# Turning the hidden blocks of five feed-forward layers on TensorE instead of VectorE and ScalarE

## The chip, the cores and the metric

The kernel runs on one core of one Trainium2 chip. The metric is the device time of one execution in microseconds (us): the median over the runs of a kernel. One further execution is recorded by the hardware profiler; its span is what the rows below count in.

## The reference, cut to what matters

Two transformer blocks of two layers each run one after the other on a sequence of 256 tokens with a width of 1024. Five times on the way stands the same gated feed-forward with a hidden width of 2816, all in float32:

```python
def swiglu_ffn(x, g, w_gate, w_up, w_down):
    h = rmsnorm(x, g)
    return (jax.nn.silu(h @ w_gate) * (h @ w_up)) @ w_down
```

The first block adds half of it to `x`, four times (two layers, ahead of and behind each mixer); the second block has it once, in its first layer. The second layer of the second block has a mixture of experts in its place. Between them stand mixers (attention and recurrences), which this change does not touch.

## The kernel before, in words

The whole network is one program. Each stage is a phase with a program written out by hand for every engine; semaphores order the engines, and a barrier of all engines ends a phase. `feed_forward` is called five times. It cuts the hidden width into 11 groups of 256 (`total = FF_PAIRS = 11`), and does two things.

**Gate and up.** For a group `c` both projections together are one block product of a 2 by 2 split: token halves (rows 0 to 127 and 128 to 255) by halves of the 1024 inputs, times input halves by (gate, up). It is done with seven products in place of eight (`P1` to `P7`), for which VectorE makes sums of weight blocks (`sum_up`, L990: four of 128x1024 for each group) and later adds the results up. Each product is four matmuls of 128 by 128 on 256 columns; each such float32 matmul is two instructions in the trace (so 8 to a product and 56 to a group, all at L878). For c > 0 the order is `P1 P6 P5 P7 P2 P4 P3`.

What the engines hand each other in a group: ScalarE copies P1 to `p1` (L941); VectorE forms `u2 = p1 + P6` (`sum_u2`, L1044), which TensorE waits for ahead of P2; `v = P7 + u2` and `up1 = P5 + v` (`sum_up1`, L1049 and L1051), which TensorE waits for ahead of P3; then in `finish` gate1 (L1055), hidden1 (L1057), up0 (L1059) and hidden0 (L1061). Hidden1 and hidden0 are silu(gate) * up, 128 tokens by 256 hidden units each, in the two halves of the tile `up`.

**The turn.** The down projection needs the hidden blocks with the hidden units on the partitions: four blocks of 128 by 128 to a group. VectorE turns the tile `up` in blocks of 32 by 32 (L1065, one instruction of 128x512), which leaves each small block turned but in its old place; ScalarE puts them into `hT` with 16 copies of a strip of 32 partitions (`place_blocks`, L931), behind its copy of P1 of the next group. Then VectorE makes four sums of turned blocks (`mix_hidden`, L1016).

**Down.** A second block product of seven products: for each of 11 groups seven matmuls on 512 columns, two instructions each (L898), summed over the groups in seven PSUM banks. Bank 7 (`TURN_BANK`) is used in the fifth feed-forward alone, by a small side product (`half_on_tensor`) at groups 1 to 4.

Weights come by DMA from the queue of SyncE, 2 MB to a group for gate and up; a slot is refilled once TensorE has finished the group that used it. TensorE transposes of 128 by 128 float32 stand elsewhere in the kernel already: at the end of a feed-forward and at the start of the next phase (`turn_block`, L658, four to a block), and in the mixers (L1576, L2261, L3150); each is one instruction in the trace.

The order of VectorE's work in a group c > 0, in which the sums are those for the next group:

```python
                sums_behind(c, 0)
                sums_behind(c, 1)
                sum_u2(c)
                sums_behind(c, 2)
                sums_behind(c, 3)
                dve.wait_ge(turned, c)
                sum_up1(c)
                mix_hidden(c - 1)
                finish(c)
```

Of the kernel before, what the change touches and what calls it, by code (L numbers as in the profile page):

```python
# [24 lines left out]
ACT = mybir.ActivationFunctionType  # L25
AX = mybir.AxisListType.X

P = 128
# [6 lines left out]
GROUP = 256  # L35
# [723 lines left out]
def feed_forward(prog, weights, gain, factor=1.0, after=(), side=None, loads=None, meanwhile=None, fresh=False, exit_gain=None, then="rows", last_norm=None):  # L759
# [11 lines left out]
    u2, v, first_gate, gate1, p1 = (mem.take(GROUP) for _ in range(5))  # L771
    up, silu, up_blocks = (mem.take(2, GROUP) for _ in range(3))
    p1_wide, u2_wide, v_wide = (Arena(prog, temps_at + i * BANK).take(BANK) for i in range(3))
# [14 lines left out]

    strip = lambda n: slice(32 * n, 32 * (n + 1))
    first_half, last_half = slice(0, KT // 2), slice(KT // 2, KT)  # L790
# [4 lines left out]
    def hidden_of(g):  # L795
        blocks = {"11": hT[:, g, 0, :], "12": hT[:, g, 1, :], "21": hT[:, g, 2, :], "22": hT[:, g, 3, :]}
        blocks.update({f"S{i + 1}": hT[:, g, 4 + i, :] for i in range(4)})
        return blocks
# [7 lines left out]
    with prog.phase() as ph:  # L806
        made, turned, acc_made, pair_used = (ph.semaphore(n) for n in ("made", "blocks_turned", "acc_made", "pair_used"))
        x_mixed_done, summed, posted, first_posted = (
# [37 lines left out]
        def _(pe):  # L846
            def gate_up(c, name):
# [32 lines left out]
                last.then_inc(made, 1)  # L880

            def down(g, name):
                left, right = factors[name]
                if g == 0:
                    if name == "P1":
                        pe.wait_ge(silu_ready, 2 * total - 1)
                    elif name == "P4":
                        pe.wait_ge(posted, posted_at(total - 1, "gate1"))
                    elif name == "P3":
                        pe.wait_ge(posted, posted_at(total - 1, "up0"))  # L890
                if name == "P1":
                    weights.wait(pe, weights.down + g)
                    pe.wait_ge(copied, g + 1)
                if name in SUM_OF:
                    pe.wait_ge(down_summed, 4 * g + SUM_OF[name])
                if name in MIX_OF:
                    pe.wait_ge(mixed, 4 * g + MIX_OF[name])
                return pe.matmul(psum[:, DOWN_BANK[name], :], hidden_of(g)[left], down_weights(g)[right],  # L898
                                 start=(g == 0), stop=(g == total - 1), skip_group_check=True)
# [5 lines left out]
            for c in range(total):  # L905
                for name in order_of(c):
                    gate_up(c, name)
            for g in range(total - 2):
                for name in PRODUCTS:
                    last = down(g, name)  # L910
                last.then_inc(pair_used, 1)
                if side and 1 <= g <= 4:
                    side.half_on_tensor(pe, g - 1, TURN_BANK)
# [11 lines left out]
        def _(act):  # L925
            def place_blocks(c):
                act.wait_ge(turned, c + 1)
                of = up_blocks.rearrange("p i (f n) -> p (i f) n", f=2)
                for m in range(4):
                    for j in range(4):  # L930
                        last = act.activation(hT[strip(m), c, 0:4, strip(j)], of[strip(j), :, strip(m)], ACT.Copy)  # L931
                last.then_inc(copied, 1)

# [5 lines left out]
            for c in range(total):  # L939
                act.wait_ge(made, made_at(c, "P1"))  # L940
                act.activation(p1, psum[:, UP_BANK["P1"], 0:GROUP], ACT.Copy).then_inc(p1_copied, 1)  # L941
                if c:
                    place_blocks(c - 1)
                    act.wait_ge(made, made_at(c, "P2"))
                    act.activation(silu[:, 0, :], psum[:, UP_BANK["P2"], 0:GROUP], ACT.Silu, scale=prog.rstd[:, 0:1]).then_inc(silu_ready, 1)
                else:
                    act.wait_ge(first_posted, 1)
                    act.wait_ge(entry.ready, 1)
                    act.activation(silu[:, 0, :], first_gate, ACT.Silu, scale=prog.rstd[:, 0:1]).then_inc(silu_ready, 1)
                act.wait_ge(posted, posted_at(c, "gate1"))  # L950
                act.activation(silu[:, 1, :], gate1, ACT.Silu, scale=prog.rstd[:, 1:2]).then_inc(silu_ready, 1)
            place_blocks(total - 1)
            if meanwhile:
# [15 lines left out]
        def _(dve):  # L969
# [83 lines left out]
            def finish(c):  # L1053
# [7 lines left out]
                dve.scalar_tensor_tensor(up[:, 0, :], up[:, 0, :], prog.rstd[:, 0:1], silu[:, 0, :], ALU.mult, ALU.mult).then_inc(posted, 1)  # L1061
                dve.wait_ge(posted, posted_at(c, "hidden0"))
                if c:
                    dve.wait_ge(copied, c)
                dve.transpose(up_blocks.rearrange("p i n -> p (i n)"), up.rearrange("p i n -> p (i n)")).then_inc(turned, 1)  # L1065

# [8 lines left out]
            for c in range(1, total):  # L1075
                sums_behind(c, 0)
                sums_behind(c, 1)
                sum_u2(c)
                sums_behind(c, 2)
                sums_behind(c, 3)  # L1080
                dve.wait_ge(turned, c)
                sum_up1(c)
                mix_hidden(c - 1)
                finish(c)
# [3487 lines left out]
```

## Time and profile before

| | |
|---|---|
| median of 3 runs | 3235.86 us (3235.29 to 3240.46) |
| time of the profiled execution | 3235.86 us |
| its span in the trace | 3234.0 us |
| mean granted TensorE clock | 0.993 of full speed |
| busy share of the span: TensorE, VectorE, ScalarE | 98%, 43%, 25% |
| gate and up, five stretches | from 11.2, 397.0, about 600, 939.8 and 1566.8 us, some 134 to 138 us each |
| down, five stretches | from 147.7, 531.4, 735.0, 1074.2 and 1705.2 us, some 66 to 75 us each |

The time of the profiled execution lies 1.9 us above its span and equals the median. In rows of the timeline the first number is the start, the second the length, both in us; instructions that follow each other are merged with their count. The length runs to the end of the last one; since matmuls overlap, what a row costs TensorE is the start of the next row less its own start. A bracket gives idle time ahead of the row and what ended it. In rows of groups, the number behind the bar is the busy time and the mean ns of one; behind the second bar stands the idle time of the engine just ahead of them.

### The profile page before, as it was taken

The numbers are of one execution on the slowest core, as the hardware profiler recorded it, in microseconds if no ns is written. First come the engines' busy times: TensorE is split into PE (matmuls) and PEld (weight loads), VectorE is DVE, ScalarE is ACT, GpSimd is POOL, SyncE is SP. The second block draws the span as 40 slices with busy tenths as digits, with TensorE's granted clock in tenths as the row PEclk, the third lists the DMA queues.
The fourth block names the chain that finished last, engine by engine and source line by source line (L and its number), as shares of the span: only waits on it lengthen the run. The fifth ranks groups of instructions, "written<-read, shape, count | busy, mean of one in ns | idle before, by whom it ended". The sixth has DMA issues, their size and how long they took to land. (4 is left out here: it accounts for less than half of the span.)

```text
span 3234.0 us, 46425 instructions
## 1 busy us (share of the span) xinstructions
PE 3157.3 (98%) x18957; PEld 1845.5 (57%) x18957; DVE 1392.8 (43%) x2513; ACT 807.6 (25%) x2139; POOL 169.0 (5%) x157
## 2 busy tenths in 40 slices
PE   8999999999999999999999999999999999999999
PEld 7845686685568567785684586864333333333333
DVE  7743386775447545633575336432112111212122
ACT  4413343351234243221352233232100000000000
POOL 0001000000000002300001104010100000000000
PEclk9999999999999999999999999999999999999999
DMA  7542045344424440134344511142899999899993
GB/s 292 195 157 105 27 160 218 131 172 161 163 75 166 182 177 27 66 115 153 153 172 153 188 56 65 54 179 87 347 382 401 393 399 399 342 393 400 392 401 134
DMA packets 81042, 665.51 MB, mean 206 GB/s; under 512 B 10528, under 2 KB 11168, under 8 KB 14016
## 3 DMA queue, kind: packets, MB, share of 16 engines
q1 hardware_dynamic: 80400, 661.31, 52.5%
q8 instruction: 152, 2.49, 0.3%
q10 hardware_dynamic: 432, 1.24, 0.1%
q14 instruction: 58, 0.48, 0.0%
HBM read 661.46 MB, written 1.05 MB: 205 GB/s over the span
## 5 line engine op out<-in xcount | busy, mean ns | idle before, releaser
L4078 PE MATMUL psum<-ring,arena 128*32 128x512 f32 x5376 | 587.8, 593 | 0.0
L878 PE MATMUL psum<-ring,arena 128*128 128x256 f32 x1760 | 398.4, 379 | 2.0 <-DVE arena L977 1.1
L4078 PEld LDWEIGHTS psum<-ring,arena 128*32 128x32 f32 x5376 | 172.3, 110 | 389.6 <-issue 388.7
L878 PEld LDWEIGHTS psum<-ring,arena 128*128 128x128 f32 x1760 | 333.8, 190 | 48.9 <-DVE ring L990 3.1
L878 PE MATMUL psum<-ring,xT_norm 128*128 128x256 f32 x1320 | 305.0, 381 | 8.9 <-DVE arena L1044 7.3
L4110 PE MATMUL psum<-ring,arena 128*32 128x512 f32 x2688 | 293.6, 592 | 0.7 <-DVE arena L4246 0.7
L878 PEld LDWEIGHTS psum<-ring,xT_norm 128*128 128x128 f32 x1320 | 251.1, 191 | 45.2 <-issue 9.2
L931 ACT ACTIVATE arena<-arena 32x128 f32<-32x128 f32 x880 | 269.5, 306 | 27.3 <-DVE arena L1065 17.7
L990 DVE TENSOR_TENSOR ring<-ring 128x1024 f32<-128x1024 f32 x220 | 266.8, 1215 | 13.2 <-DMA ring<-in_ffn_w 6.8
L4242 DVE TENSOR_TENSOR arena<-arena,psum 128x256 f32<-128x256 f32 x84 | 35.5, 423 | 411.0 <-ACT arena L4216 411.0
L898 PE MATMUL psum<-ring,arena 128*128 128x512 f32 x440 | 205.8, 592 | 0.0
L4110 PEld LDWEIGHTS psum<-ring,arena 128*32 128x32 f32 x2688 | 88.2, 110 | 200.5 <-issue 191.2
L2972 PE MATMUL psum<-xT_norm,ring 128*128 128x256 f32 x832 | 184.4, 380 | 0.0
L4254 DVE TENSOR_TENSOR arena<-arena,psum 128x512 f32<-128x512 f32 x156 | 107.7, 690 | 157.4 <-PE psum L4110 157.4
L2972 PEld LDWEIGHTS psum<-xT_norm,ring 128*128 128x128 f32 x832 | 157.1, 190 | 25.3 <-issue 4.9
L898 PE MATMUL psum<-arena 128*128 128x512 f32 x330 | 157.9, 592 | 0.0
L898 PEld LDWEIGHTS psum<-ring,arena 128*128 128x128 f32 x440 | 83.3, 190 | 101.2 <-issue 100.9
L4216 ACT ACTIVATE arena<-psum 128x256 f32<-128x256 f32 x84 | 32.5, 386 | 420.7 <-PE psum L4078 420.7
L4188 ACT ACTIVATE arena<-psum 128x384 f32<-128x384 f32 x28 | 13.8, 493 | 419.7 <-PE psum L4091 419.7
L898 PEld LDWEIGHTS psum<-arena 128*128 128x128 f32 x330 | 62.4, 190 | 77.0 <-issue 76.3
L1001 DVE TENSOR_TENSOR arena<-ring 128x512 f32<-128x512 f32 x55 | 40.0, 728 | 122.0 <-PE psum L898 122.0
L3666 PE MATMUL psum<-ring,xT_norm 128*128 128x256 f32 (+1 forms) x256 | 84.6, 486 | 0.0
(594 smaller groups left out, 3504.0 us busy)
## 6 DMA issues: line engine op xcount, KB each, us to landing
ring<-in_moe_w SPq DMA_DIRECT2D x340, 1024.0 KB, 7.2
ring<-in_ffn_w SPq DMA_DIRECT2D x50, 2048.0 KB, 7.6
ring<-in_ffn_w SPq DMA_DIRECT2D x65, 1024.0 KB, 4.9
ring<-in_merge_w SPq DMA_DIRECT2D x16, 2048.0 KB, 8.3
ring<-in_feat_w SPq DMA_DIRECT2D x12, 2048.0 KB, 8.7
ring<-in_ev_in_w SPq DMA_DIRECT2D x4, 2048.0 KB, 9.0
ring<-in_od_in_w SPq DMA_DIRECT2D x4, 2048.0 KB, 9.4
ring<-in_merge_w SPq DMA_DIRECT2D x8, 1024.0 KB, 11.6
```

The costliest lines, as they stand in the source:

```text
L878: last = pe.matmul(psum[:, bank, 0:GROUP], a[:, k, :], w[:, k, :], start=(fresh and k == 0), stop=(k == KT // 2 - 1), skip_group_check=True)
L898: return pe.matmul(psum[:, DOWN_BANK[name], :], hidden_of(g)[left], down_weights(g)[right], start=(g == 0), stop=(g == total - 1), skip_gr ...
L931: last = act.activation(hT[strip(m), c, 0:4, strip(j)], of[strip(j), :, strip(m)], ACT.Copy)
L990: dve.tensor_tensor(w[out], w[a], w[b], ALU.subtract).then_inc(summed, 1)
L1001: dve.tensor_tensor(w[out], w[a], w[b], ALU.subtract).then_inc(down_summed, 1)
L2972: last = pe.matmul(psum[:, s % 4, x * S:(x + 1) * S], weights[:, i, (f + x) * P:(f + x + 1) * P], prog.xT[:, i, :], start=(i == 0), stop=( ...
L3666: last = pe.matmul(gate_bank(m)[:, at:at + w.shape[2]], prog.xT[:, k, b * P:(b + 1) * P], w[:, k, :], start=(k == 0), stop=(k == KT - 1))
L4078: last = pe.matmul(psum[part(j), r, :], xg[:, u.i, u.group // GROUPS, r * P + BLOCK * j:r * P + BLOCK * (j + 1)], m[:, j, :], start=(u.i = ...
L4110: last = pe.matmul(psum[part(j), down_bank(n, r), :], hT[:, c, r * P + BLOCK * j:r * P + BLOCK * (j + 1)], m[:, j, :], start=(c == 0), sto ...
L4216: act.activation(silu[:, r, :], psum[:, r, 0:S], ACT.Silu).then_inc(silu_ready, 1)
L4242: dve.tensor_tensor(hidden[:, r, :], silu[:, r, :], psum[:, r, S:2 * S], ALU.mult).then_inc(hidden_ready, 1)
L4254: last = dve.tensor_tensor(at, at, psum[:, down_bank(n, r), :], ALU.add)
```

## The change

The turn moves to TensorE. For each group `turn(c)` transposes the four blocks of `up` into bank 7 with four TensorE transposes, and one ScalarE copy of 128x512 (`copy_turned`) takes them to `hT`. The turn of group c - 1 stands behind P6 of group c; that of the last group stands behind the fourth product (P7) of the first down group. VectorE's block transpose, the 16 strip copies of ScalarE and the tile `up_blocks` go. The wait on `copied`, which guarded `up_blocks`, now guards bank 7. In VectorE's order `mix_hidden(c - 1)` moves ahead of the fourth sum and of `sum_up1`. The blocks "12" and "21" of `hT` change places, since the copy keeps the order of the transposes. In the fifth feed-forward TensorE also waits for the last copy out of bank 7 before the side product uses it.

```diff
-    up, silu, up_blocks = (mem.take(2, GROUP) for _ in range(3))
+    up, silu = mem.take(2, GROUP), mem.take(2, GROUP)
...
-        blocks = {"11": hT[:, g, 0, :], "12": hT[:, g, 1, :], "21": hT[:, g, 2, :], "22": hT[:, g, 3, :]}
+        blocks = {"11": hT[:, g, 0, :], "21": hT[:, g, 1, :], "12": hT[:, g, 2, :], "22": hT[:, g, 3, :]}
...
+            def turn(c):
+                pe.wait_ge(posted, posted_at(c, "hidden0"))
+                if c:
+                    pe.wait_ge(copied, c)
+                for t in range(2):
+                    for i in range(2):
+                        last = pe.transpose(psum[:, TURN_BANK, (2 * t + i) * P:(2 * t + i + 1) * P], up[:, i, t * P:(t + 1) * P],
+                                            prog.ident)
+                last.then_inc(turned, 1)
...
                 for name in order_of(c):
                     gate_up(c, name)
+                    if c and name == "P6":
+                        turn(c - 1)
             for g in range(total - 2):
-                for name in PRODUCTS:
+                for n, name in enumerate(PRODUCTS):
                     last = down(g, name)
+                    if g == 0 and n == 3:
+                        turn(total - 1)
                 last.then_inc(pair_used, 1)
+                if side and g == 1:
+                    pe.wait_ge(copied, total)
...
-            def place_blocks(c):
+            def copy_turned(c):
                 act.wait_ge(turned, c + 1)
-                of = up_blocks.rearrange("p i (f n) -> p (i f) n", f=2)
-                for m in range(4):
-                    for j in range(4):
-                        last = act.activation(hT[strip(m), c, 0:4, strip(j)], of[strip(j), :, strip(m)], ACT.Copy)
-                last.then_inc(copied, 1)
+                act.activation(hT[:, c, 0:4, :].rearrange("p j t -> p (j t)"), psum[:, TURN_BANK, :], ACT.Copy).then_inc(copied, 1)
...
                 if c:
-                    place_blocks(c - 1)
+                    copy_turned(c - 1)
...
-                dve.wait_ge(posted, posted_at(c, "hidden0"))
-                if c:
-                    dve.wait_ge(copied, c)
-                dve.transpose(up_blocks.rearrange("p i n -> p (i n)"), up.rearrange("p i n -> p (i n)")).then_inc(turned, 1)
...
                 sum_u2(c)
                 sums_behind(c, 2)
+                mix_hidden(c - 1)
                 sums_behind(c, 3)
-                dve.wait_ge(turned, c)
                 sum_up1(c)
-                mix_hidden(c - 1)
                 finish(c)
```

## Rows read from the trace of the kernel before

**Rows 1.** The page, granted TensorE clock in 40 slices of the span, tenths.

```profile
PEclk9999999999999999999999999999999999999999
```

**Rows 2.** Costliest groups by line, whole span: gate and up, strip copies, block transpose.

```profile
L878 PE MATMUL psum<-ring,arena 128*128 128x256 f32 x1760 | 398.4, 379 | 2.0 <-DVE arena L977 1.1 <-DVE ring L990 0.9
...
L878 PE MATMUL psum<-ring,xT_norm 128*128 128x256 f32 x1320 | 305.0, 381 | 8.9 <-DVE arena L1044 7.3 <-DMA ring<-in_ffn_w 1.6
...
L931 ACT ACTIVATE arena<-arena 32x128 f32<-32x128 f32 x880 | 269.5, 306 | 27.3 <-DVE arena L1065 17.7
...
L1065 DVE STREAM_TRANSPOSE arena<-arena 128x512 f32<-128x512 f32 x55 | 39.1, 711 | 1.9
```

**Rows 3.** Timeline, second feed-forward, group 2 to the start of group 3.

```profile
422.65 1.89 PE L878 MATMUL psum<-ring,xT_norm 128*128 128x256 f32 x8
...
423.31 0.49 DVE L1061 SCALAR_TENSOR_TENSOR arena<-arena,norm_stats 128x256 f32<-128x256 f32 x1
...
424.37 5.34 PE L878 MATMUL psum<-ring,arena 128*128 128x256 f32 x24
...
429.55 3.62 PE L878 MATMUL psum<-ring,xT_norm 128*128 128x256 f32 x16
...
434.73 1.46 PE L878 MATMUL psum<-ring,xT_norm 128*128 128x256 f32 x6
```

**Rows 4.** Timeline, TensorE around the four transposes in the first feed-forward's end.

```profile
208.60 0.60 PE L658 MATMUL psum<-constants,x_resid 128*128 128x128 f32 x4
209.04 3.60 PE L898 MATMUL psum<-ring,arena 128*128 128x512 f32 x8
```

**Rows 5.** Timeline, TensorE around 32 transposes in a mixer, and what follows.

```profile
1295.89 3.66 PE L3150 MATMUL psum<-constants,ring 128*96 128x128 f32 x32
1300.66 1.13 PE L2187 MATMUL psum<-arena 64*128 64x256 f32 x8 [1.11 <-PEq L377]
```

**Rows 6.** Windows: length, TensorE busy and instructions, granted clock, DMA share, GB/s.

```profile
1300.00:1305.00 5.00, 4.34 (x33) 1.00 0.69 244
...
1590.00:1592.00 2.00, 2.00 (x6) 0.50 0.00 0
```

**Rows 7.** Timeline, four transposes between short products in a mixer.

```profile
1349.34 0.66 PE L2261 MATMUL psum<-constants,ring 128*128 128x128 f32 x4
1350.11 0.59 PE L2221 MATMUL psum<-arena 128*128 128x192 f32 x2
```

**Rows 8.** Timeline, second feed-forward, group 1.

```profile
410.86 5.34 PE L878 MATMUL psum<-ring,arena 128*128 128x256 f32 x24
410.92 0.49 DVE L1061 SCALAR_TENSOR_TENSOR arena<-arena,norm_stats 128x256 f32<-128x256 f32 x1
...
412.07 4.84 DVE L990 TENSOR_TENSOR ring<-ring 128x1024 f32<-128x1024 f32 x4
...
416.83 0.41 DVE L1044 TENSOR_TENSOR arena<-arena,psum 128x256 f32<-128x256 f32 x1
...
417.39 3.69 PE L878 MATMUL psum<-ring,xT_norm 128*128 128x256 f32 x16 [1.19 <-DVE arena L1044]
...
420.01 0.42 DVE L1051 TENSOR_TENSOR arena<-psum,arena 128x256 f32<-128x256 f32 x1
420.35 1.14 DVE L1016 TENSOR_TENSOR arena<-arena 128x128 f32<-128x128 f32 x4
420.92 1.89 PE L878 MATMUL psum<-ring,arena 128*128 128x256 f32 x8
```

**Rows 9.** Timeline, fifth feed-forward, group 1.

```profile
1582.97 0.49 DVE L1061 SCALAR_TENSOR_TENSOR arena<-arena,norm_stats 128x256 f32<-128x256 f32 x1
...
1588.88 0.42 DVE L1044 TENSOR_TENSOR arena<-arena,psum 128x256 f32<-128x256 f32 x1
...
1589.44 5.38 PE L878 MATMUL psum<-ring,xT_norm 128*128 128x256 f32 x16 [2.08 <-DVE arena L1044]
1594.66 1.67 PE L878 MATMUL psum<-ring,arena 128*128 128x256 f32 x7
```

**Rows 10.** Timeline, fifth feed-forward's side product: ScalarE copy of a PSUM bank.

```profile
1719.10 0.60 ACT L4399 ACTIVATE arena<-psum 128x512 f32<-128x512 f32 x1 [6.92 <-PE psum L4392]
```

More of the change, by code:

```diff
@@ L787, in down_weights @@
         return {"11": w[:, 0, 0], "12": w[:, 0, 1], "21": w[:, 1, 0], "22": w[:, 1, 1], "T1": s1, "T2": s2, "T3": w[:, 0, 1], "T4": s4}
-    strip = lambda n: slice(32 * n, 32 * (n + 1))
     first_half, last_half = slice(0, KT // 2), slice(KT // 2, KT)
@@ L806, in feed_forward @@
     with prog.phase() as ph:
-        made, turned, acc_made, pair_used = (ph.semaphore(n) for n in ("made", "blocks_turned", "acc_made", "pair_used"))
+        made, turned, acc_made, pair_used = (ph.semaphore(n) for n in ("made", "hidden_turned", "acc_made", "pair_used"))
         x_mixed_done, summed, posted, first_posted = (
@@ L951, in _ @@
                 act.activation(silu[:, 1, :], gate1, ACT.Silu, scale=prog.rstd[:, 1:2]).then_inc(silu_ready, 1)
-            place_blocks(total - 1)
+            copy_turned(total - 1)
             if meanwhile:
```

## The prediction, made before the changed kernel ran

> **What bounds the kernel now.** I read the page first, for the shares and the clock; then the groups by line, for what ended TensorE's idle time in the feed-forwards; then the timeline of one feed-forward, for the order inside a group; then rows of transposes elsewhere, for the price of a turn. The granted clock is at nine tenths or more of full speed in every slice [rows 1]. In gate and up, TensorE issued 3080 instructions (1760 and 1320) and sat idle for only 2.0 + 8.9 = 10.9 us ahead of them, over all five feed-forwards; 7.3 us of this were ended by VectorE's u2 at L1044 [rows 2]. The reader should see how little there is to win there. A settled group shows it from inside: P1 of group 2 starts at 422.65 and P1 of group 3 at 434.73, so a group takes 12.08 us; the first product takes 424.37 - 422.65 = 1.72 us, and seven of these are 12.06 us [rows 3]. TensorE does not stop within a group, and this holds for the groups behind it too, since the 7.3 us are five waits, one in each feed-forward, all in group 1 (1.65, 1.19, 1.19, 1.18 and 2.08 us; two of the five stand in [rows 8, 9]). The down products follow the same way without a stop.
>
> So VectorE's block transpose (55 of 0.711 us) and the 880 strip copies of ScalarE (269.5 us in all) [rows 2] lie beside TensorE's work, except where they push u2 of group 1 back. What is put on TensorE, on the other hand, lies on the path.
>
> **What is added to TensorE.** Eleven turns in each of five feed-forwards, 55 in all, of four transposes: 220 instructions. The kernel has the same four transposes between two runs of matmuls: they start at 208.60, the next matmul at 209.04 [rows 4]. A turn therefore takes 0.44 us of TensorE, or 0.11 us for a transpose. The length of one in that row (0.60 us for four) contains a tail that overlaps with the next matmul and is not paid. Thirty-two in a row took 3.66 us with the tail [rows 5], 0.11 each again. For a lower bound I take 0.43 (a quarter of the product's 1.72 us, since a turn streams 512 columns once where a product streams 1024 twice); for an upper one the widest that four transposes have between short products in a mixer, 1350.11 - 1349.34 = 0.77 us [rows 7], where some of it may be a wait. I take 0.44, since those neighbours are long matmul runs as here. 55 x 0.44 = 24.2 us.
>
> The Trainium skill ("TensorE: Matmul & The Clock Gate", Part 4: PE-mode transpose) gives about 275 ns for a 128x128 transpose inside a kernel. By that the 220 would be an estimated 60 us. The spacing in the rows above speaks for the smaller number: the page's figure is near the length of a single one here, not near the distance to the next.
>
> **Does the turn wait?** It needs hidden0 of the group before, posted at 423.31 + 0.49 = 423.80; P6 ends at 424.37 + 1.72 = 426.09 [rows 3]. It has 2.3 us to spare, and the wait costs nothing. If it were late, P5 and all behind it would be. The copy out of bank 7 is long done by the next turn.
>
> **ScalarE.** Sixteen strips of 0.306 us, 4.9 us a group, become one copy from PSUM of 0.60 us [rows 10]. Nothing on TensorE waited for the strips, so this is worth nothing but free time.
>
> **VectorE.** The transpose goes; this frees 412.07 - 411.41 = 0.66 us ahead of the sums, of which 0.03 stay as the usual gap: 0.63. In a settled group it buys nothing. `mix_hidden` now stands ahead of the fourth sum. It waits for the copied blocks: turn until 426.53, about 0.2 for the signal, 0.60 for the copy, 427.3. VectorE gets there after u2 (from about 426.3, for 0.41) and a sum of 1.21 (a quarter of 4.84 [rows 8]), at 427.9. Behind it stand the fourth sum and v and up1, for which P3 waits: 427.9 + 1.05 + 1.21 + 0.45 + 0.42 = 431.1, but v needs P7 (out at 426.53 + 3.44 + 0.2 = 430.2), so about 431.1 either way; P3 is due at 426.53 + 4 x 1.72 = 433.4. It is 2.3 us early. The move is free there.
>
> **Group 1, where VectorE is late.** In the second feed-forward P7 of group 1 ends at 410.86 + 3 x 1.72 = 416.0, and P2 starts at 417.39, behind u2 (posted 417.24) [rows 8]. After the change: P6 ends at 412.58, hidden0 was posted at 411.41, the turn runs to 413.02, P7 ends at 416.46. VectorE's four sums start at 411.44; u2 starts 0.63 earlier, at 416.20, is posted at 416.61, and P2 starts at 416.76. The turn is hidden in the old wait, and 0.63 us more is gained. But next comes P3, which waits for up1. VectorE: sum until 417.75, mix_hidden occupying 421.40 - 420.35 = 1.05 until 418.8, sum until 420.0, v and up1 until 420.87, so P3 starts at 421.02 instead of 420.92 [rows 8]; TensorE would be ready at 416.76 + 3.53 = 420.29. The moved mix_hidden gives the gain back as a new wait of 0.7 us. Net for group 1: +0.10 us instead of +0.44. From group 2 on VectorE has caught up. A feed-forward costs 10 x 0.44 + 0.10 = 4.5 us; four cost 18.0.
>
> **The fifth.** There the first weights came late, and TensorE idled enough for its granted clock to fall to 0.50, that is 1.2 GHz, just behind the wait of 2.08 us [rows 6, 9]: the 16 instructions of P2 and P4 took 1594.66 - 1589.44 = 5.22 us where they take 3.53 in [rows 8]. With the turn, TensorE works until about 1587.5 (turn behind hidden0, 1583.46 + 0.15 + 0.44, then P5 and P7), and P2 starts 0.64 earlier, at 1588.8: an idle of 1.3 us, about that of the feed-forwards in which the clock held. I take it that it holds. Then P3 waits for up1, 4.26 us behind u2 as in group 1 above: 1588.66 + 4.26 + 0.15 = 1593.1, which is 1.6 earlier. If the clock falls all the same, 0.6 earlier. So 4.4 - 1.6 = 2.8 us.
>
> **Sum.** 18.0 + 2.8 = +20.8 us on the profiled execution of 3235.86, which is also the median: 3256.7 us. Queues are not passed: no DMA is added or moved, SyncE starts each weight load behind the same products, and loads start later with TensorE itself. The last turn stands in the first down group, behind the fourth product. A down product streams half the columns of one of gate and up, so four are 4 x 0.86 = 3.4 us behind the last P3, while hidden0 comes 1.15 us behind it (423.80 less 422.65 [rows 3]); the turn does not wait. The added wait of the side product is for a copy many us old.
>
> **The rivals.**
>
> A. A turn costs more than 0.44 (switching from matmuls to transposes and back, loading `up` as weights between short matmuls of 256 columns). For: in a mixer four took 0.77 [rows 7]. Against: [rows 4]. At 0.77: (50 x 0.77) + 0.5 - 1.6 = 37 us, 3273 us. Halfway, 0.60: 28.5 us, 3264.
>
> B. The clock suffers. If transposes did not keep the clock up, the turn and the wait of group 1 would together let it fall in the other four feed-forwards as in the fifth, at 5.22 - 3.53 = 1.7 us each, and in the fifth as well, where 1.0 us of the gain is lost: +7.8, 3264.5 us. Against: 32 transposes alone, from 1295.89, with 1.11 us of idle behind them, left the clock at 1.00 in the next 5 us [rows 5, 6]. The Trainium skill ("TensorE: Matmul & The Clock Gate", Part 4) says that the full clock does not engage for transposes, which do not count as busy in the same way; by that rule this rival would hold, and the trace does not agree with it.
>
> C. The other side: not slower. TensorE's time is regained from somewhere. The waits of group 1 are worth 7.3 us, all counted; even with all 10.9 us of idle gone, 24.2 - 10.9 = +13.3. Only the clock is large enough: a mean of 0.993 over 3234 us is 22.6 us that could at most be missing. If the shifted phases met no low clock anywhere, the time would be 24.2 - 22.6, about 3237.5 us; it decides from 14.4 regained beyond my sum. Against: the low stretches lie nearly all in mixers, which the change only moves.
>
> D. Milder: `mix_hidden` early does not delay up1 in group 1, so that P3 follows at once: -0.7 in each, 3253.2 us.
>
> **How the numbers follow.** My forecast 0.70; A 0.10; B 0.04; C 0.05; D 0.11. 0.2% of the median is 6.5 us, about what a measurement of this kernel can tell from no change. The forecast, A, B and D are slower: 0.95. C lies within 0.2% at its own price, but reaches to both sides of it. I give 0.93 to slower, 0.05 to the same and 0.02 to faster, which leaves 0.02 for the low end of the others, should a turn and the clock both come out cheap. The range: down to D and a further 3 us for clock phases, 3250; up to the half-way case of A and B, 3265.
>
> **What the profile after would show.** 220 TensorE instructions at the new transpose line, started about 0.11 us apart, and the product behind each turn 0.44 us after it began; groups of 12.5 us in place of 12.08; no row of the block transpose, 55 ScalarE copies of some 0.6 us; the idle ended by L1044 down from 7.3 us to about 2 us, and a new one of about 0.7 us in each group 1 ended by the up1 line; in the fifth feed-forward no stretch at 0.50. The prediction is wrong if the gap of a turn is clearly above or below 0.44, if P5 or P3 waits in settled groups, or if stretches outside the feed-forwards change their length by several us.

## The result, and the profile after

| | before | after |
|---|---|---|
| median, runs side by side | 3239.0 us (5 runs, 3235.29 to 3241.51) | 3267.56 us (5 runs, 3257.35 to 3277.86) |
| profiled execution, its span | 3235.86, 3234.0 us | 3268.03, 3266.2 us |
| mean granted clock of that execution | 0.993 | 0.990 |
| busy TensorE, VectorE, ScalarE (page) | 3157.3, 1392.8, 807.6 us | 3192.1, 1358.0, 575.7 us |

The ratio is 1.0088, with a 95% interval of 1.0058 to 1.0116. The change makes the kernel slower, as forecast, but by more than the range allowed: 3267.56 lies above 3265. With these five runs the record holds thirteen more executions of the kernel after; all eighteen have a median of 3267.4 us.

The groups by line of the kernel after answer to [rows 2]. The new instructions are the transposes (L887) and the 55 copies of a bank (L943); the gate and up product stands at L877 now.

```profile
L877 PE MATMUL psum<-ring,arena 128*128 128x256 f32 x1760 | 406.7, 379 | 2.2 <-DVE arena L1062 1.7 <-DVE ring L1001 0.5
L877 PE MATMUL psum<-ring,xT_norm 128*128 128x256 f32 x1320 | 304.9, 381 | 3.0 <-DMA ring<-in_ffn_w 1.7 <-DVE arena L1055 1.3
...
L887 PE MATMUL psum<-constants,arena 128*128 128x128 f32 x220 | 33.1, 273 | 0.3 <-DVE arena L1072 0.3
...
L943 ACT ACTIVATE arena<-psum 128x512 f32<-128x512 f32 x55 | 32.9, 597 | 112.2 <-PE psum L887 112.2
```

The wait for u2 (now L1055) fell from 7.3 to 1.3 us; the one for up1 (L1062), 1.7 us, is new. The timeline of the second feed-forward, from P6 of group 1 to P6 of group 3, answers to [rows 3, 8]:

```profile
416.34 1.89 PE L877 MATMUL psum<-ring,arena 128*128 128x256 f32 x8
...
418.06 0.60 PE L887 MATMUL psum<-constants,arena 128*128 128x128 f32 x4
418.50 3.62 PE L877 MATMUL psum<-ring,arena 128*128 128x256 f32 x16
...
421.58 0.41 DVE L1055 TENSOR_TENSOR arena<-arena,psum 128x256 f32<-128x256 f32 x1
...
422.14 3.69 PE L877 MATMUL psum<-ring,xT_norm 128*128 128x256 f32 x16
423.05 1.14 DVE L1027 TENSOR_TENSOR arena<-arena 128x128 f32<-128x128 f32 x4
...
425.69 0.42 DVE L1062 TENSOR_TENSOR arena<-psum,arena 128x256 f32<-128x256 f32 x1
...
426.17 1.99 PE L877 MATMUL psum<-ring,arena 128*128 128x256 f32 x8 [0.34 <-DVE arena L1062]
...
428.00 1.89 PE L877 MATMUL psum<-ring,xT_norm 128*128 128x256 f32 x8
...
429.73 1.89 PE L877 MATMUL psum<-ring,arena 128*128 128x256 f32 x8
...
431.45 0.60 PE L887 MATMUL psum<-constants,arena 128*128 128x128 f32 x4
431.89 3.62 PE L877 MATMUL psum<-ring,arena 128*128 128x256 f32 x16
...
442.25 1.89 PE L877 MATMUL psum<-ring,arena 128*128 128x256 f32 x8
```

The turn takes 431.89 - 431.45 = 0.44 us, and a group 442.25 - 429.73 = 12.52 us in place of 12.08. Group 1 hides its turn: from P6 (416.34) to the next P1 (428.00) it is 11.66 us, where it was 422.65 - 410.86 = 11.79.

Stage by stage, from the first and the last TensorE row of each stage in the two traces:

| us | before | after | difference |
|---|---|---|---|
| gate and up, five feed-forwards | 136.42, 134.38, 134.38, 134.37, 138.39 | 139.94, 138.21, 138.22, 138.22, 141.15 | +17.8 |
| down, five | 67.13, 67.13, 67.13, 66.26, 74.00 | 67.57, 67.57, 67.57, 66.69, 74.44 | +2.2 |
| first and second mixer | 182.26, 137.70 | 183.57, 142.73 | +6.3 |
| between fourth and fifth feed-forward | 426.35 | 429.36 | +3.0 |
| start; behind the fifth | 11.24; 1449.94 | 11.44; 1452.56 | +2.8 |

The lengths are from this one trace of each kernel. The feed-forwards, where all of the change is, account for 20.0 us of the 32.2. The other 12.2 us came in stages whose code did not change. The windows show what part of that is (length, busy time and instructions of TensorE, weight loads, VectorE, ScalarE, GpSimd, granted clock, DMA share, GB/s). The kernel after, in its second mixer:

```profile
916.00:918.00 2.00, 2.00 (x11) 2.00 (x11) 0.00 (x0) 1.19 (x2) 0.00 (x0) 0.50 0.04 8
918.00:920.00 2.00, 2.00 (x12) 2.00 (x11) 0.00 (x0) 0.00 (x0) 0.00 (x0) 0.50 0.00 0
```

The kernel before, at the same work:

```profile
902.00:904.00 2.00, 2.00 (x21) 2.00 (x20) 0.00 (x0) 0.94 (x2) 0.00 (x0) 1.00 0.04 8
```

The two timelines show that the work and the idle time ahead of it are alike. Before, then after:

```profile
901.19 1.07 PE L1269 MATMUL psum<-constants,arena 128*128 128x128 f32 x8 [1.14 <-ACT arena L1358]
902.10 3.68 PE L1282 MATMUL psum<-arena 128*128 128x64 f32 x32
```

```profile
915.32 1.75 PE L1275 MATMUL psum<-constants,arena 128*128 128x128 f32 x8 [1.14 <-ACT arena L1364]
916.85 6.93 PE L1288 MATMUL psum<-arena 128*128 128x64 f32 x32
```

The same 1.14 us of idle, the same 40 instructions: once at full clock, once at half. I summed (1 - granted clock) over windows of 2 us through both traces: 23.6 us lost before, 31.8 after. The losses come in pieces of 1.7 us or multiples. The second mixer has one piece before (1.7 us) and 6.8 us after. So 8.2 us of the growth between these two traces is low clock, net of 1.7 us that the fifth feed-forward gained.

### The profile page after: what moved, and what is told of

Its sections match the earlier page's. It is cut to its first block and busy times, and to the rows that moved or that the text cites. A ratio compares the mean times of both kernels' runs of the same rounds, so it can differ in the third digit from the quotient of the medians.

```text
span 3266.2 us, 45985 instructions
## 1 busy us (share of the span) xinstructions
PE 3192.1 (98%) x19177; PEld 1873.0 (57%) x19177; DVE 1358.0 (42%) x2458; ACT 575.7 (18%) x1314; POOL 169.1 (5%) x157
## 3 DMA queue, kind: packets, MB, share of 16 engines
HBM read 661.46 MB, written 1.05 MB: 203 GB/s over the span
## 5 line engine op out<-in xcount | busy, mean ns | idle before, releaser
L877 PE MATMUL psum<-ring,arena 128*128 128x256 f32 x1760 | 406.7, 379 | 2.2 <-DVE arena L1062 1.7
L877 PEld LDWEIGHTS psum<-ring,arena 128*128 128x128 f32 x1760 | 330.0, 190 | 47.2 <-DVE arena L1062 3.7
L877 PE MATMUL psum<-ring,xT_norm 128*128 128x256 f32 x1320 | 304.9, 381 | 3.0 <-DMA ring<-in_ffn_w 1.7
L877 PEld LDWEIGHTS psum<-ring,xT_norm 128*128 128x128 f32 x1320 | 251.0, 191 | 39.6 <-issue 3.2
L907 PE MATMUL psum<-ring,arena 128*128 128x512 f32 x440 | 206.6, 592 | 0.0
L2978 PEld LDWEIGHTS psum<-xT_norm,ring 128*128 128x128 f32 x832 | 156.7, 190 | 25.2 <-issue 4.6
L4222 ACT ACTIVATE arena<-psum 128x256 f32<-128x256 f32 x84 | 32.4, 386 | 420.7 <-PE psum L4084 420.7
L3711 PE MATMUL psum<-ring,arena 128*128 128x512 f32 x192 | 83.2, 593 | 0.0
```

What stands on the lines that cost most here:

```text
L877: last = pe.matmul(psum[:, bank, 0:GROUP], a[:, k, :], w[:, k, :], start=(fresh and k == 0), stop=(k == KT // 2 - 1), skip_group_check=True)
L2978: last = pe.matmul(psum[:, s % 4, x * S:(x + 1) * S], weights[:, i, (f + x) * P:(f + x + 1) * P], prog.xT[:, i, :], start=(i == 0), stop=( ...
L3711: last = pe.matmul(branch_bank(n), oT[:, turned_order.index(x), k, b * P:(b + 1) * P], w[:, j, k, :], start=(k == 0), stop=(k == 3))
```

## The experiments

The questions: is the price inside the feed-forwards the turn's; is the rest tied to the turn, to any delay, or to chance; and was there a time to be had from the wait for u2. In the table the third column is the ratio to the kernel before on the same chip with its 95% interval.

| kernel | median us (runs) | ratio | before beside it |
|---|---|---|---|
| before again | 3243.02 (12) | 1.0018 [0.9996, 1.0041] | 3238.91 (20) |
| after again, 1st | 3269.17 (6) | 1.0105 [1.007, 1.0139] | 3238.91 |
| after again, 2nd | 3268.33 (6) | 1.0078 [1.0063, 1.0094] | 3241.0 (17) |
| after again, 3rd | 3270.46 (6) | 1.0105 [1.0069, 1.0142] | 3238.13 (23) |
| turns alone | 3263.99 (9) | 1.0069 [1.0042, 1.0095] | 3238.91 |
| mix_hidden put back | 3269.53 (6) | 1.009 [1.0061, 1.0118] | 3238.91 |
| one transpose for four | 3248.47 (12) | 1.0022 [1.0007, 1.0037] | 3241.0 |
| delay of 1.7 us in one place | 3245.12 (12) | 1.0012 [0.9993, 1.003] | 3239.34 (24) |
| delay of 3.5 us in one place | 3244.96 (11) | 1.002 [1.001, 1.0029] | 3239.34 |
| delay of 20 us in one place | 3259.67 (5) | 1.0072 [1.0058, 1.0086] | 3239.34 |
| the same again | 3260.74 (10) | 1.0062 [1.0042, 1.0081] | 3238.13 |
| delay of 4.1 us in each feed-forward | 3266.64 (6) | 1.0081 [1.0059, 1.0103] | 3241.0 |
| the same again | 3262.13 (8) | 1.0071 [1.0038, 1.0104] | 3238.13 |
| u2 early in group 1 | 3227.01 (6) | 0.9966 [0.9955, 0.9978] | 3239.34 |
| the same again | 3231.24 (12) | 0.997 [0.9952, 0.9989] | 3238.13 |
| GpSimd later by one memset | 3269.16 (8) | 1.0104 [1.006, 1.0148] | 3240.9 (9) |
| GpSimd later by six memsets | 3266.92 (6) | 1.0091 [1.006, 1.0121] | 3241.47 (11) |

### The two kernels again

> The kernel before, unchanged, for the spread of its time. Theory P (the feed-forwards cost what the turns cost, some 20 us, and the rest of the 28 us comes from where the granted clock falls to one half in stages that the change does not touch): the runs of this kernel scatter as well, by several pieces of 1.7 us, and time less the time lost to the half clock is constant within 1 us. Theory S (something in the change makes the untouched stages slower): all runs stay within 3235 to 3242 us.

> The changed kernel, unchanged, for its spread and a second trace. Theory P: the stretches of gate and up and of down have the same lengths as in the first trace (138.2 and 67.6 us, within 0.2), and the untouched stages have other lengths than in it, by pieces of 1.7 us. Theory S: the untouched stages are again about 12 us longer than in the kernel before, in the same places.

> The changed kernel once more, for the spread, beside the pure delay on the same chip. Median 3265 to 3269 if what was seen holds; 3260 to 3263 if the earlier medians were high by luck.

> The changed kernel once more beside both delays: mean of the kernel before plus 26 to 28.

Both medians came back. The stretches of gate and up and of down repeated within 0.02 us in the second to fourth feed-forward and within 0.4 us in the first; the first mixer took 182.26 and 185.04 us in two executions of the kernel before, and 183.57, 189.09, 179.03 and 188.98 in four of the kernel after. The scatter of a run is thus outside the feed-forwards, in the mixers for the most part; once, in the second repeat, the stretch behind the fifth feed-forward took 17 us more. All 121 runs of the kernel before together have a median of 3240.9 us and reach from 3231.2 to 3266.3, and the three runs shown ahead of the prediction were 5 us below that median. The 36 executions of the kernel after (the eighteen of the result and three repeats of six) have 3268.9. The third repeat was expected 26 to 28 us above the kernel before; by its mean it was 32.9 us above it on the same chip.

### The turns alone

This is the kernel before, with its block transpose and strip copies; the transposes go to bank 7, where nobody reads them.

```diff
+            def turn(c):
+                pe.wait_ge(posted, posted_at(c, "hidden0"))
+                for t in range(2):
+                    for i in range(2):
+                        pe.transpose(psum[:, TURN_BANK, (2 * t + i) * P:(2 * t + i + 1) * P], up[:, i, t * P:(t + 1) * P],
+                                     prog.ident)
...
+                    if c and name == "P6":
+                        turn(c - 1)
```

> The kernel before with the 55 turns added on TensorE at the same places, their result unused; VectorE's block transpose and ScalarE's strips stay. Theory P: 54 or so settled turns of 0.44 us; in group 1 the turn hides in the wait for u2. Each feed-forward grows by 10 x 0.44 = 4.4 us, 22 in all, 3258 us give or take the clock; no group shorter. Rival (the changed time is made by the moved VectorE and ScalarE work): under 10 us.

The down group got the same turn behind its fourth product. The timeline of this kernel, around the turn of group 1 in the second feed-forward:

```profile
424.22 0.60 PE L886 MATMUL psum<-constants,arena 128*128 128x128 f32 x4
424.65 3.62 PE L878 MATMUL psum<-ring,arena 128*128 128x256 f32 x16
...
429.01 3.69 PE L878 MATMUL psum<-ring,xT_norm 128*128 128x256 f32 x16 [0.74 <-DVE arena L1055]
```

The turn is 0.43 us again, and the old wait for u2 shrinks from 1.19 to 0.74 us by the length of the turn. A feed-forward (second to fourth) became 3.95 + 0.44 = 4.4 us longer; the change's own are 3.84 + 0.44 = 4.3. So the turns on TensorE make the price inside the feed-forwards. The rest of the change has two parts there that nearly cancel, as the next kernel shows.

### mix_hidden put back behind sum_up1

An edit of the kernel after:

```diff
-                mix_hidden(c - 1)
                 sums_behind(c, 3)
                 sum_up1(c)
+                mix_hidden(c - 1)
```

> The changed kernel with mix_hidden back behind sum_up1. The wait of P3 in group 1 goes (0.34 us and 0.1 at the restart), since up1 no longer stands behind mix_hidden: each feed-forward 0.4 us shorter, 2 us in all, hidden in the scatter of the total but to be seen in the stretches: gate and up 137.8 us instead of 138.2. If mix_hidden's move were what makes the change dear, 5 us or more would go.

The timeline of this kernel, group 1 of the second feed-forward from the turn on:

```profile
413.69 0.60 PE L887 MATMUL psum<-constants,arena 128*128 128x128 f32 x4
414.13 3.62 PE L877 MATMUL psum<-ring,arena 128*128 128x256 f32 x16
...
417.77 3.69 PE L877 MATMUL psum<-ring,xT_norm 128*128 128x256 f32 x16
...
421.30 1.89 PE L877 MATMUL psum<-ring,arena 128*128 128x256 f32 x8
```

P3 follows P4 at once; the wait of 0.34 us is gone, and gate and up takes 137.61 us in place of 138.21. The moved `mix_hidden` costs 0.6 us in each of these feed-forwards, where 0.4 was expected: P3 starts 3.53 us behind P2 in place of 4.03, and the next P1 1.73 us behind P3 in place of 1.83. Without the move a feed-forward would be (137.61 - 134.38) + 0.44 = 3.7 us dearer than before, against 4.4 with the turns alone. So taking the transpose off VectorE gave 0.7 us back in group 1, and the move of `mix_hidden` spent 0.6 of it. The median did not fall with it: its 3 us drown in the mixers' scatter at six runs.

### One transpose in place of four

For every group but the first of a feed-forward the turn holds one transpose. This kernel leaves out the other three, so three of the four hidden blocks of such a group are not turned; the waits are unchanged. An edit of the kernel after:

```diff
-                for t in range(2):
-                    for i in range(2):
+                for t in range(1 if c else 2):
+                    for i in range(1 if c else 2):
```

> The changed kernel with one transpose in place of four in every turn but the first of a feed-forward; the other three blocks of each are left as they were, so this part of the hidden values is not computed. ScalarE's copy, VectorE's order and all waits stay. If the transposes are the cost, 50 x 3 x 0.11 = 16 us go: a settled group of 12.19 us instead of 12.52, 3252 us against 3268. If the switch between matmuls and transposes, or the wait, is the cost, little goes, and a turn still takes 0.3 us or more.

The timeline of this kernel, the turn in a settled group:

```profile
433.93 0.27 PE L887 MATMUL psum<-constants,arena 128*128 128x128 f32 x1
434.04 3.62 PE L877 MATMUL psum<-ring,arena 128*128 128x256 f32 x16
```

A lone transpose between long products takes 434.04 - 433.93 = 0.11 us, a quarter of 0.44: the rows show no cost of switching. The five feed-forwards are 16.1 us shorter in this trace than with four transposes, where 50 x 3 x 0.11 = 16.5 were expected; the median fell by 20.4 us from the 3268.9 of the kernel after, and the rest of that is within the scatter. The length of the lone transpose in its row is 0.27 us.

The Trainium skill ("TensorE: Matmul & The Clock Gate", Part 4: PE-mode transpose) gives about 275 ns, measured with bf16; in these float32 rows this is near the length, while the distance to the next instruction, 0.11 us, is what TensorE pays.

### Delays without the change

Filler matmuls on zeros into the free bank 7, by the kernel's own function `stay_busy`, are put into the kernel before behind P7 of the first down group: 8, 16 and 93 of them in the second feed-forward alone, then 19 in each of the five (without the last condition of the edit shown, and in the first behind a wait for the constants' load). Their result is not used.

```diff
-                for name in PRODUCTS:
+                for n, name in enumerate(PRODUCTS):
                     last = down(g, name)
+                    if g == 0 and n == 3 and weights is prog.shifted:
+                        stay_busy(prog, pe, TURN_BANK, 8)
```

> The kernel before with 8 small matmuls (128x512, bf16, of zeros) put in once, behind the fourth product of the first down group of the second feed-forward, before all the mixers but the first: a pure delay of 8 x 0.216 = 1.7 us, no other work changed. Theory P (where the granted clock falls depends on when a stage comes, and on luck from run to run): the later stages keep their work and idle, but pieces of 1.7 us come and go in them; time less 1.7 lies between 3232 and 3264 with a median that may be some us off 3241. Theory S (the later stages are slower in the changed kernel because of its turns): median 3242.5, the later stages as in the kernel before.

> The same with 16 matmuls, a delay of 3.5 us. Theory P as for 1.7 us. Theory S: median 3244.5.

> The same with 93 matmuls, a delay of 20.1 us, the size of what the turns cost in the feed-forwards. If the 7 to 10 us above the turns' price come with any delay of this size, the median is 3266 to 3270 as in the changed kernel; if they hang on the turns or the freed engines, it is 3259 to 3262; if luck alone made them, either.

> The delay of 20.1 us in one place once more. Mean of the kernel before plus 20 to 22 if the first five runs hold; plus 24 or more if they were low by luck and any late mixer pays.

> The kernel before with a pure delay of 19 x 0.216 = 4.1 us in each of the five feed-forwards, 20.5 in all, behind the fourth product of the first down group, so that every later stage comes about as late as in the changed kernel. If the 6 to 7 us that the changed kernel has above its feed-forwards' 20 come from when the mixers come (where the clock falls), the median is 3266 to 3270; if they hang on the transposes or on the freed engines, or are luck of the runs, it is 3260 to 3263.

> The pure delay of 4.1 us in each feed-forward once more, for a mean over twice as many runs. If the time above the delay comes with the delay itself, the mean stays 4 to 8 us above that of the kernel before plus 20.5; if the first six runs were high by luck, it falls to within 2 us of it.

The traces show the delays at their size: the down stretches grew by 1.73, 3.46, 20.07 and five times 4.10 us. The medians alone leave the matter open: against the kernel before on the same chip they grew by 20.3 and 22.6 us for the 20.1 us in one place, and by 25.6 and 24.0 for the 20.5 in five. Each run also comes with its mean granted clock, and time times clock is the time that it would have taken had no clock been lost. (Low clock behind the last matmul counts here too, though TensorE does nothing there; in the first two traces this is 1.3 and 1.1 us.) The clock is rounded to a thousandth (3.2 us), so only means over many runs count. Means with their standard errors:

| us | runs | mean time | time x clock | lost to low clock |
|---|---|---|---|---|
| before | 116 | 3241.6 | 3211.8 ± 0.1 | 29.8 ± 0.7 |
| after (all on record) | 36 | 3269.5 | 3237.1 ± 0.2 | 32.4 ± 1.5 |
| of these, the three repeats | 18 | 3272.1 | 3237.2 ± 0.3 | 34.9 ± 2.1 |
| turns alone | 9 | 3266.6 | 3236.5 ± 0.4 | 30.2 ± 3.6 |
| 1.7 us in one place | 12 | 3243.9 | 3215.0 ± 0.2 | 28.9 ± 1.2 |
| 3.5 us in one place | 11 | 3245.0 | 3217.5 ± 0.4 | 27.4 ± 1.1 |
| 4.1 us in each feed-forward | 14 | 3265.9 | 3236.0 ± 0.4 | 29.9 ± 2.5 |
| 20.1 us in one place | 15 | 3260.7 | 3235.5 ± 0.4 | 25.2 ± 1.0 |
| u2 early | 18 | 3230.7 | 3205.4 ± 0.3 | 25.3 ± 1.3 |

The change adds 25.3 ± 0.2 us of work and waits at full clock. The feed-forwards account for 20.0 of it and for 1.7 more that the fifth paid before as low clock; 3.6 us lie outside. Pure delays show the same kind of surcharge: 1.7 us put in become 3.2, 3.5 become 5.7, 20.1 become 23.7, and 20.5 become 24.2. So a surcharge of 1.5 to 3.7 us comes with a delay, without any transpose. With the turns alone 2.0 us lie outside. The traces show one place of it: with the low clock taken off, the stretch between the fourth and the fifth feed-forward took 424.6 and 423.3 us in two executions of the kernel before, 425.8 to 426.2 in four of the kernel after, and 425.5 to 427.0 in four with the large delays.

The low clock decides less than the repeats alone suggest. They lost 5.1 ± 2.2 us more than the kernel before; all 36 executions lost 2.6 ± 1.7 us more, which is not clear of zero. The five delays show no difference to the kernel before, the single one of 20.1 us lost 4.6 ± 1.2 less. What makes the clock fall in one execution and not in another is not shown.

### VectorE and GpSimd in the last mixer

One part outside the feed-forwards was the same in all six traces in which VectorE's and ScalarE's part of the turn had been changed and nothing was put ahead of GpSimd's product, and in none of the eleven traces of the kernel before, of the turns alone, of the delays and of the early u2. In the last mixer VectorE and GpSimd each multiply a tile of 128x1536 at the same time. The timeline of the kernel before:

```profile
1947.25 1.76 DVE L3485 TENSOR_TENSOR ring<-ring,arena 128x1536 f32<-128x1536 f32 x1
1947.38 4.24 POOL L3353 TENSOR_TENSOR ring<-ring,arena 128x1536 f32<-128x1536 f32 x1 [37.08 <-DVE arena L3482]
```

The kernel after, with the product of TensorE that waits for VectorE's next step:

```profile
1976.75 2.76 POOL L3359 TENSOR_TENSOR ring<-ring,arena 128x1536 f32<-128x1536 f32 x1 [37.08 <-DVE arena L3488]
1976.96 4.15 DVE L3491 TENSOR_TENSOR ring<-ring,arena 128x1536 f32<-128x1536 f32 x1 [0.46 <-DVE arena L3488]
...
1989.47 3.85 PE L3018 MATMUL psum<-arena,constants 8*128 8x256 f32 x11 [1.32 <-DVE arena L3497]
```

GpSimd is first by 0.21 us here; its product takes 2.76 us instead of 4.24 and VectorE's 4.15 instead of 1.76. TensorE then waits 1.32 us where it waited 0.26. Two kernels put memsets of an unused column ahead of GpSimd's product, to turn the order round, the first with the one line shown, the second with six of it:

```diff
             pool.wait_ge(squared, SQUARES["k"])
+            do(pool.memset(prog.spare, 0.0))
             do(tt(k_mla, k_mla, spread(kept.qk_stat[:, 1].unsqueeze(3), TB, NH8, QK), ALU.mult))
```

> The changed kernel with one tiny GpSimd memset (one column of a spare tile) ahead of GpSimd's product of 128x1536 in the last mixer, so that GpSimd starts it a few tenths of a us later and VectorE's product of the same shape starts first, as in the kernel before. If who starts first decides, VectorE's takes 1.76 us again instead of 4.15, GpSimd's about 4.2 instead of 2.8, TensorE's wait behind it 0.26 instead of 1.32, and the stretch behind the last feed-forward is 1.1 us shorter, 2.8 where a half-clock piece goes with it. If the length comes from something else (where the tiles lie), it stays 4.15.

> The kernel after, with six tiny GpSimd memsets of one unused column ahead of GpSimd's first product in the last mixer (one cost 0.18 us, so GpSimd starts some 0.9 us later than with one). Theory of the start order (whichever of the two starts its product first runs undisturbed, the other is drawn out): VectorE's product takes 1.76 us again in place of 4.15 to 4.31, GpSimd's first product is drawn out from 2.76 to about 4.2 us, TensorE's wait behind the next VectorE step falls from 1.32 to about 0.3 us, and the median falls by 1 us, or by up to 2.8 us if a half-clock piece goes with it (some 3266 to 3268). Rival (VectorE is slow there for another reason, such as what it did before): VectorE's product stays above 4 us although it starts first, TensorE's wait stays 1.3 us, and the median stays at about 3269.

One memset did not do it: GpSimd started at 1973.41, VectorE at 1973.47 and took 4.31 us, so that run said nothing. Six did. The timeline of that kernel:

```profile
1978.02 1.76 DVE L3498 TENSOR_TENSOR ring<-ring,arena 128x1536 f32<-128x1536 f32 x1 [0.46 <-DVE arena L3495]
...
1978.73 3.65 POOL L3366 TENSOR_TENSOR ring<-ring,arena 128x1536 f32<-128x1536 f32 x1
...
1989.46 4.61 PE L3019 MATMUL psum<-arena,constants 8*128 8x256 f32 x16 [0.26 <-DVE arena L3504]
```

VectorE's product is back at 1.76 us, TensorE's wait at 0.26, the low clock behind it at 3.4 us in place of the 5.1 of the kernel after, and everything behind the fifth feed-forward took 1450.56 us against 1452.56. The start order is shown to be the cause of 1.1 us. The 1.7 us of clock went in this one execution, so that part is likely, not shown: of the seven traces with the slow product five lost 5.1 and two 3.4, of the twelve with the quick one none lost more than 3.4. Of the 2.8 us in all, 0.8 came back in small steps elsewhere in the stretch. The median of 3266.92 us is too scattered (3260.45 to 3287.8) to show 2 us. The numbers fit a wait of the second until the first is done: 0.71 us after VectorE's start GpSimd would wait out 1.05 and then need 2.76, 3.81 in all, measured 3.65. In the kernel before the same sum gives 4.39 for GpSimd (measured 4.24), in the kernel after 4.31 for VectorE (4.15), with one memset 4.46 (4.31).

The Trainium skill ("SBUF — State Buffer", section "SBUF: two separate sides") says that a VectorE instruction with two SBUF inputs and a GpSimd one that reads SBUF exclude each other for the whole instruction, and that whichever starts first gets the shared ports; the rows agree to 0.15 or 0.16 us in all four cases.

Why VectorE started 0.46 us behind its reciprocal in the kernels with the changed work of VectorE and ScalarE, and 0.11 in the others, stays open. It is neither the delay nor the transposes, since with either of them alone it was 0.11.

### u2 early in group 1

The prediction had found 7.3 us of waits for u2 in the kernel before. This kernel takes them without moving the turn: in group 1 VectorE makes u2 ahead of the weight sums, and up1 ahead of the last two.

```diff
             for c in range(1, total):
+                if c == 1:
+                    sum_u2(c)
                 sums_behind(c, 0)
                 sums_behind(c, 1)
-                sum_u2(c)
+                if c == 1:
+                    dve.wait_ge(turned, c)
+                    sum_up1(c)
+                else:
+                    sum_u2(c)
                 sums_behind(c, 2)
                 sums_behind(c, 3)
-                dve.wait_ge(turned, c)
-                sum_up1(c)
+                if c > 1:
+                    dve.wait_ge(turned, c)
+                    sum_up1(c)
```

> The kernel before (VectorE's turn) with another order in group 1 alone: u2 ahead of the sums for the next group, v and up1 behind two of them. TensorE's wait for u2 (7.3 us in five places) goes: P2 follows P7 at once, 1.4 us earlier in each of the second to fourth feed-forwards, 1.9 in the first, 2.3 plus 1.7 of clock in the fifth; 9 to 10 us in all, if up1 is in time for P3: 3231 us against 3241, give or take the clock. If VectorE is only late elsewhere instead, under 3 us.

> The kernel before with u2 early in group 1, once more: mean 9 to 12 us below the kernel before.

The timeline of this kernel, group 1 of the second feed-forward, answers to [rows 8]:

```profile
405.82 5.34 PE L878 MATMUL psum<-ring,arena 128*128 128x256 f32 x24
...
409.39 0.41 DVE L1044 TENSOR_TENSOR arena<-arena,psum 128x256 f32<-128x256 f32 x1
...
411.00 3.62 PE L878 MATMUL psum<-ring,xT_norm 128*128 128x256 f32 x16
```

P2 follows P7 without a wait. Gate and up became 132.96 us from 134.38 in three feed-forwards, 134.94 from 136.42 in the first, and 134.21 from 138.39 in the fifth, where the half-clock stretch of [rows 6] went too: 9.9 us, and the mean over 18 runs fell by 10.9: 6.4 us at full clock and 4.5 as low clock. It beats both kernels.

## Why the prediction was right and where it failed

**The turn's price** was right: 0.44 us, 220 transposes 0.11 apart, groups of 12.52 us, the last turn in the down group 0.43 or 0.44. Rival A (0.77, or 0.60) is refuted by the timeline and by the kernel with one transpose.

**Group 1** was right in kind. The turn is hidden, u2's wait nearly went, and a wait for up1 came, of 0.34 us where 0.7 was worked out; VectorE's path from P6 to the end of up1 took 9.77 us in place of 10.01, and P3 followed up1 by 0.06 us in place of 0.15. P3 starts 9.83 us behind P6 (426.17 - 416.34), not 10.16. The group gained 0.13 where it was to lose 0.10. So the group came out 0.23 us better than forecast, a third of the 0.7 of rival D. Putting `mix_hidden` back shows that its move costs 0.6 us in a feed-forward; in settled groups it is free, as said.

**The fifth feed-forward**: +2.76 and +0.44 = 3.2, where 2.8 was forecast. Its clock held behind P2's wait of 1.10 us, as this row and these windows of the kernel after show:

```profile
1615.68 3.69 PE L877 MATMUL psum<-ring,xT_norm 128*128 128x256 f32 x16 [1.10 <-DVE arena L1055]
```

```profile
1614.00:1616.00 2.00, 0.90 (x5) 0.50 (x4) 2.00 (x3) 0.00 (x0) 0.00 (x0) 1.00 0.02 8
1616.00:1618.00 2.00, 2.00 (x11) 1.77 (x10) 1.93 (x6) 0.32 (x1) 0.00 (x0) 1.00 0.00 0
```

A turn waited there once, for 0.25 us (the 0.3 at L887). Rival B is refuted: no window of a feed-forward of the kernel after is below full clock.

**The sum over the feed-forwards**, +20.8, measured +20.0. This part of the sum held to 0.8 us.

**What failed first is the base.** The sum was added to 3235.86, "the profiled execution ... which is also the median". Three runs close together looked like a sharp base; 121 runs have a median of 3240.9. That is 5.0 us of the miss of 10.9 (3267.56 - 3256.7), or 3.1 by the five runs beside it.

**What failed second is the term for everything outside the feed-forwards**, set to nothing in the sum and to "a further 3 us for clock phases" in the range, and on the lower side only. Rival C had the place (the low stretches lie in mixers, which the change "only moves") and looked at a gain alone. The mean time grew by 27.9 ± 1.7 us; less the 20.0, 7.9 us came outside the feed-forwards where nothing was forecast: 3.6 at full clock, and 4.3 (2.6 and the fifth's 1.7) as low clock, with a standard error of 1.7.

Of the 3.6, 1.1 us is the start order of VectorE and GpSimd, shown. The other 2.5 us are of the size that the delays and the turns alone bring too (1.5 to 3.7), so stages whose code is the same take other times when they are moved, and no transpose is needed for it; which instruction tips it is not shown. The prediction had named such lengths outside the feed-forwards as a sign that it is wrong. The 4.3 us of low clock stay open. The runs do not even settle that the change as a whole loses more clock than the kernel before, nor that it differs from the five delays (29.9 ± 2.5 against 32.4 ± 1.5).

## What to carry to other kernels

Moving work to the engine that bounds the kernel costs its spacing in the stream, here 0.11 us for a 128x128 transpose and not the 0.27 us of its row, and what it replaces is worth no more than the waits that it pushed back, here 0.7 us in a feed-forward. Before moving work, ask whether the small wait that one hopes to win can be had by reordering: three moved lines took 10 us here. A change of under 1% in a kernel with clock dips in other stages needs a base of many runs, and a forecast of it needs a term with both signs for the stages that are merely moved; time times granted clock, averaged, separates the two to 0.3 us.

## What the runs showed of the hardware

- Gate and up of the second to fourth feed-forward, where TensorE hardly stops, repeated within 0.02 us from one execution to the next; the first mixer with the same code took between 178.6 and 189.2 us.
- Clock was lost in pieces of 1.7 us or multiples, nearly all outside the feed-forwards, 20 to 47 us in a profiled execution. The longest stretch at half clock lasted 37 us, once in the kernel after and once with the turns alone. This row is from the second repeat of the kernel after (2110 to 2120 us); TensorE was 100% busy in it and stayed at half clock all the same:

```profile
2110.00:2120.00 10.00, 10.00 (x53) 0.50 0.00 0
```

- 32 transposes with 1.11 us of idle behind them [rows 5, 6], and turns in every group, left the granted clock at 1.00.
- Two products of 128x1536, one on VectorE (1.76 us alone) and one on GpSimd (2.76 us alone), started 0.06 to 0.71 us apart: the second to start took 3.65 to 4.31 us.
